# The four loads of a coming head pair, issued at four points of a recurrence period

## The chip, the cores and the metric

The kernel runs on one core of one Trainium2 chip. The metric is the device time of a launch in microseconds, from the core's own counters; smaller is better. Engines are named as in the profile: PE is TensorE, DVE is VectorE, ACT is ScalarE, POOL is GpSimd, SP is SyncE, whose queue issues nearly all DMAs here.

## The reference, cut to what matters

Two residual layers over x of 512 tokens by 1024 channels, float32. Layer 0 mixes by a convolution module and differential attention, layer 1 by a bidirectional RWKV-7 recurrence; each layer adds a cross attention into 256 memory tokens and a squared-ReLU MLP of 4096. The change lies in the recurrence of layer 1:

```python
def step(S, inp):
    r_t, w_t, k_t, v_t, a_t, b_t = inp
    sa = jnp.einsum('bhij,bhj->bhi', S, a_t)
    S = S * w_t[:, :, None, :] + sa[..., None] * b_t[:, :, None, :] + v_t[..., None] * k_t[:, :, None, :]
    return S, jnp.einsum('bhij,bhj->bhi', S, r_t)

y_f = wkv7_scan(r, decay[0], k_dir[0], v, -kk, kk * a_rate[0], reverse=False)
y_b = wkv7_scan(r, decay[1], k_dir[1], v, -kk, kk * a_rate[1], reverse=True)
```

There are 16 heads of 64 channels, and a forward and a backward scan.

## The kernel before

All other stages are dense products with weights streamed from HBM. The recurrence (`stage_wkv`) is done in chunks of 64 tokens, and for two heads at a time: a pair p (0 to 7) is 128 channels, one partition each. Before this stage r, the normalised k (called kk), k and v of all pairs have been written to HBM. `load_pair` (L1988 to L1991) brings the four 128x512 tiles of one pair into `pin[:, p % 2, a, :]`, with a = 0 for r, 1 for kk, 2 for k and 3 for v. Each tile is one DMA of 256 KB, and each raises the semaphore `s_pin[p % 2]` by 16. Two pairs have room at a time.

The work of a pair is spread over three periods. `SCAN_PERIOD` is a list of steps, each with a lag: in period t, the step "QB-1" is QB of pair t - 1 and "VT-0" is VT of pair t. `scan_order` (L2012) writes the list out, and every engine runs through the same order and does its own steps of it, in order. Steps in capitals are PE's. Steps in small letters that bear the name of a PE step take its result out of PSUM: ua, ub, vt on ACT, qb and bn on DVE. The steps that matter here, in PE's order within a period:

- UB-2, W-0, HK-2, GA-2, Z00-1, GB-2, HU-2, QB-1, Z01-1, X00-1, C1-2, X01-1, VT-0, TK-1, TB-1, Z11-1 and on. Z and X are the products of the blockwise inverse of pair t - 1, C1 to C6 the chunk chain of pair t - 2.
- VT (L2295 to L2302) centres and transposes v of pair t: eight matmuls with v of `pin` as weights. Ahead of it PE waits for the whole pair:

```python
elif kind == "VT":
    pe.wait_ge(s_half, 1)
    pe.wait_ge(s_pin[b], 64 * (p // 2 + 1))
```

- ua-2 and ub-2 (ACT, L2540) come at the beginning of the period. qb-1 (DVE, L2665) comes in the order right before VT-0.
- d0-0 and d2-0 (DVE, L2596 and L2630) read r and kk later in the period, d1 (L2619) reads k at the beginning of the next, bs (POOL, L2256) reads r and bn (DVE, L2646) reads v still later. d0, d1 and d2 wait for the same count of `s_pin` as VT.
- QB is `s_k_scores` in the rows, and its copy qb is the DVE instruction `s_k_scores<-ps,con` of L2665. VT is `ps<-s_centre,pair_in` of L2300.

SP's queue in period t (`scan_sp`), in order: at vt-0 it waits for vt, and for Y of pair t - 2, which PE ends with YS near the end of the period; then it issues four v_rows DMAs (L2209), four small lora loads (L1985), the store of y of pair t - 2 (L2221), and at bn-1 the store of the bonus of pair t - 1 (L2214) and the four loads of pair t + 1 (L1991). The tiles of pairs 0 and 1 are loaded ahead of the stage, all four together.

Of the kernel before, what the change touches and what calls it, by code (L numbers as in the profile page):

```python
# [30 lines left out]
C = D // P  # L31
# [74 lines left out]
class Kernel:  # L106
# [43 lines left out]
    def sb(self, name, shape, ctx=None, dt=F32):  # L150
        return (ctx or self.ctx).enter_context(self.nc.sbuf_tensor(name, shape, dt))
# [1456 lines left out]
def stage_rwkv_in(k):  # L1608
# [4 lines left out]
    with ExitStack() as cx:  # L1613
# [52 lines left out]
        def rin_sp(sp):  # L1666
            sp.dma_start(k.d_memt, k.memt[:, :, :]).then_inc(s_mtout, 16)
            k.load_weights(sp, sm + 4)
            sp.dma_start(k.d_h, h[:, :, :]).then_inc(s_hout, 16)
            k.load_weights(sp, at_end)  # L1670
            sp.wait_ge(s_hout, 16)
            sp.wait_ge(s_mtout, 16)

            sp.wait_ge(s_x, 48)
            sp.dma_start(k.mv_t[:, :, :], k.d_memt).then_inc(k.s_mv_in, 16)
            sp.dma_start(k.mv_w[:, :, :], k.i["xattn_w_kv"][1][:, 2 * D - SLOT:2 * D].rearrange("(k p) n -> p k n", p=P)) \
              .then_inc(k.s_mv_in, 16)
            for p in range(2):
                load_lora(k, sp, p)
            for c in range(8):  # L1680
                k.wait_freed(sp, num[("v", c)])
                sp.dma_start(k.d_v[:, c, :], sv[:, c % 2, :]).then_inc(s_vout[c % 2], 16)
                if c in (2, 5):
                    half = slice(4 * (c // 3), 4 * (c // 3) + 4)
                    sp.wait_ge(s_kk, half.stop)
                    sp.dma_start(k.d_kk[:, half, :], kk[:, half, :]).then_inc(s_kout, 16)
                elif c in (3, 4):

                    p = c - 3
                    k.wait_full(sp, num["k", 7])  # L1690
                    sp.wait_ge(s_kout, 16)
                    sp.wait_ge(s_out[p], 16 * 5)
                    sp.wait_ge(s_vout[p], 16)
                    load_pair(k, sp, p)
# [285 lines left out]
def load_lora(k, sp, p):  # L1980

    halves = (slice(0, CH), slice(CH, P))
    for a, src in enumerate((k.i["rwkv_w2"], k.i["rwkv_a2"])):
        for z in range(2):
            sp.dma_start(k.lora[halves[z], p % 2, a, :], src[0, z, :, p * P:(p + 1) * P]).then_inc(k.s_lora[p % 2], 16)  # L1985


def load_pair(k, sp, p):  # L1988

    for a, src in enumerate((k.d_r, k.d_kk, k.d_k, k.d_v)):  # L1990
        sp.dma_start(k.pin[:, p % 2, a, :], src[:, p, :]).then_inc(k.s_pin[p % 2], 16)  # L1991


# [63 lines left out]
def stage_wkv(k, proj):  # L2057
# [10 lines left out]
    with ExitStack() as cx:  # L2068
# [13 lines left out]
        ua = sb("a_rows_u", [P, NC, 2, 2, CH])  # L2082
# [67 lines left out]
        def full(eng, kind, p):  # L2150

            j = job[kind, p]
            eng.wait_ge(s_full[j % 2], j // 2 + 1)

        def taken(eng, kind, p):

            j = job[kind, p]
            eng.wait_ge(s_taken[j % 2], j // 2 + 1)

        def last_of(kinds, p):  # L2160
            return max(kinds, key=lambda n: job[n, p])
# [28 lines left out]
        def scan_sp(sp, gate):  # L2190
            for wait in k.scan_inputs:

                sp.wait_ge(*wait)
            for kind, p in order:
                if kind == "mv":
                    if p == 7:
                        sp.wait_ge(s_mvt, 2)
                        sp.dma_start(k.d_vv[1][:, :, 3 * SLOT:D], mvs).then_inc(s_mvo, 16)
                elif kind == last_of(("W", "A"), p) and p + 2 < C:
                    full(sp, kind, p)  # L2200
                    load_lora(k, sp, p + 2)
                elif kind == "vt":
                    taken(sp, "VT", p)
                    if p >= 2:
                        full(sp, "Y", p - 2)
                        sp.wait_ge(s_hf, p - 1)
                    for z in range(2):
                        for e in range(2):
                            sp.dma_start(vr[HP[z], p % 2, e::2].rearrange("p c h t -> p c (h t)"), vs[HP[e], :, :]) \  # L2209
                              .then_inc(s_vd, 16)  # L2210
                elif kind == "bn":
                    taken(sp, "BN", p)
                    if p < C - 1:
                        sp.dma_start(k.d_bon[:, p, :], bon[:, :]).then_inc(s_bo, 16)  # L2214
                    if p + 2 < C:
                        full(sp, "VT", p)
                        load_pair(k, sp, p + 2)
                elif kind == "ya":
                    if p < C - 1:
                        taken(sp, "Y", p)  # L2220
                        sp.dma_start(k.d_y[:, p, :], yb[:, p % 2, :]).then_inc(s_yo[p % 2], 16)  # L2221
                elif kind == "ly":
                    for b in range(2):
                        sp.wait_ge(s_yo[b], 32 if p == 0 else 64 - 16 * b)
                    gate.load_y(sp, p)
                elif kind == "lb":
                    taken(sp, last_of(("GA", "GB"), p + 6), p + 6)
                    sp.wait_ge(s_bo, 64 if p == 0 else 112)
                    gate.load_bonus(sp, p)
                elif kind == "lg":  # L2230
                    full(sp, "BN", 7)
                    gate.load_g2(sp)
                elif kind == "lw":
                    if p == 2:
                        taken(sp, last_of(("GA", "GB"), 7), 7)
                    elif p == 3:
                        gate.wait_g2(sp)
                    k.load_weights(sp, gate.first + p)
# [335 lines left out]
        def scan_dve(dve, gate):  # L2574
# [9 lines left out]
            for kind, p in order:  # L2584
# [122 lines left out]
                elif kind[0] == "c":  # L2707
# [5 lines left out]
                    else:  # L2713
# [4 lines left out]
                                      view(ends, 0, [[1, 2], [0, CH]]), ALU.mult).then_inc(s_sn, 1)  # L2718

    return Scan(proj, [x for x in order if x not in LEAD], scan_sp, scan_pe, scan_act, scan_dve, scan_pool, bon, lambda eng: taken(eng, "Y", C - 1),  # L2720
                lambda eng: taken(eng, "BN", C - 1), lambda eng: eng.wait_ge(s_y0, C))

# [246 lines left out]
```

## Time and profile before

| | |
|---|---|
| time, 3 runs | 1931.05 us median (1930.81 to 1932.45) |
| the profiled execution's own time | 1928.18 us |
| its span, first to last instruction | 1926.4 us |
| mean granted TensorE clock | 0.994 |
| PE busy | 1859.2 us (97%) |
| DVE busy | 1055.7 us (55%) |
| the stretch from 980 to 1380 us, with the recurrence | PE 384.8 of 400 us, DVE 309.2 us |

The span is one execution on the chip. A busy PE counts matmuls whose ends are modelled, so that it may hold short waits. "issue" as a releaser means that nothing in the profile explains the wait. DMA queue q1 holds all DMAs that SP issued, q8 and q14 the loads of instructions.

### The profile page before, as it was taken

How to read it: one execution, taken by the hardware profiler on the slowest of the kernel's cores; microseconds unless marked ns; L12 is line 12 of the kernel's file. 1: busy time of each engine (PE TensorE's matmuls, PEld its weight loads, DVE VectorE, ACT ScalarE, POOL GpSimd, SP SyncE). 2: the span in 40 equal slices, each digit the busy share in tenths (PEclk: the TensorE clock that was granted, in tenths of full speed). 3: DMA queues.
4: the chain of work that ended last, by engine and by line, in shares of the span. 5: the costliest groups of instructions: out<-in, count | busy, mean ns of one | idle time of the engine just before them, and what ended most of it. 6: DMA issues, size and time to landing. Idle time of an engine off the chain costs nothing.

```text
span 1926.4 us, 38666 instructions
## 1 busy us (share of the span) xinstructions
PE 1859.2 (97%) x17053; PEld 1529.8 (79%) x17053; DVE 1055.7 (55%) x1405; ACT 755.4 (39%) x1006; POOL 174.2 (9%) x136
## 2 busy tenths in 40 slices
PE   6999899999999999999999999999999999999997
PEld 4898558778888888775679898899787788888886
DVE  5897665444432443447648888787664344324422
ACT  4434674334421332323844343343643353213322
POOL 1000002000000000210003211111120010000000
PEclk9999999999999999999999999999999999999999
DMA  6227223112332232443441111112352132332221
GB/s 213 84 72 233 77 99 131 66 44 91 106 110 87 88 110 90 153 137 126 153 140 50 50 50 51 50 47 69 125 197 88 33 99 87 110 103 88 94 88 44
DMA packets 165503, 189.41 MB, mean 98 GB/s; under 512 B 11801, under 2 KB 152646, under 8 KB 163674
## 3 DMA queue, kind: packets, MB, share of 16 engines
q1 hardware_dynamic: 162016, 174.44, 28.2%
q0 software_dynamic: 3088, 12.45, 1.6%
q8 instruction: 135, 2.21, 0.5%
q14 instruction: 30, 0.25, 0.0%
q10 hardware_dynamic: 234, 0.06, 0.0%
HBM read 161.22 MB, written 21.51 MB: 95 GB/s over the span
## 4 chain that ended last, share of the span: by engine, by line
PE 48%; DVE 5%; issue 2%; ACT 2%; DMA 0%; ACTq 0%; DVEq 0%; SPq 0%
PE ps L357 10%; PE ps L359 10%; PE ps L358 10%; PE ps L2353 7%; PE ps L2319 2%; PE ps L2366 2%; PE ps L2307 1%; PE ps L1743 1%; PE ps L2330 1%; PE ps L1313 1%; PE ps L2412 1%; PE ps L2449 1%; PE ps L1294 1%; DVE s_inverse_t L2683 1%; PE ps L2286 1%
## 5 line engine op out<-in xcount | busy, mean ns | idle before, releaser
L344 DVE TENSOR_TENSOR weights_split<-w,weights_split 128x2048 fp32r<-128x2048 f32 x116 | 265.7, 2290 | 235.3 <-ACT weights_split L326 230.5
L326 ACT ACTIVATE weights_split<-w 128x2048 fp32r<-128x2048 f32 x118 | 225.5, 1911 | 288.7 <-PE ps L359 270.2
L357 PE MATMUL ps<-x_hn_hi,weights_split 128*128 128x512 f32 x640 | 252.7, 395 | 0.0
L359 PE MATMUL ps<-x_hn_hi,weights_split 128*128 128x512 f32 x640 | 249.2, 389 | 0.0
L358 PE MATMUL ps<-x_hn_lo,weights_split 128*128 128x512 f32 x640 | 249.0, 389 | 0.0
L357 PE MATMUL ps<-f_hidden_hi,weights_split 128*128 128x512 f32 x512 | 199.3, 389 | 0.0
L359 PE MATMUL ps<-f_hidden_hi,weights_split 128*128 128x512 f32 x512 | 199.2, 389 | 0.0
L358 PE MATMUL ps<-f_hidden_lo,weights_split 128*128 128x512 f32 x512 | 199.2, 389 | 0.0
L1563 DVE SCALAR_TENSOR_TENSOR f_relu<-ps,x_squares 128x512 f32<-128x512 f32 x64 | 44.1, 691 | 191.1 <-PE ps L359 172.5
L358 PEld LDWEIGHTS ps<-x_hn_lo,weights_split 128*128 128x128 f32 x640 | 120.2, 188 | 26.2 <-issue 1.4
L357 PEld LDWEIGHTS ps<-x_hn_hi,weights_split 128*128 128x128 f32 x640 | 120.2, 188 | 26.0 <-issue 1.4
L359 PEld LDWEIGHTS ps<-x_hn_hi,weights_split 128*128 128x128 f32 x640 | 120.1, 188 | 25.3
L462 POOL TENSOR_TENSOR x_squares<-x_squares 128x512 f32<-128x512 f32 x36 | 50.5, 1401 | 948.3 <-ACT x_squares L454 947.6
L1447 ACT ACTIVATE f_squared<-f_relu 128x512 f32<-128x512 f32 x64 | 40.4, 631 | 200.7 <-DVE f_relu L1563 200.7
L358 PEld LDWEIGHTS ps<-f_hidden_lo,weights_split 128*128 128x128 f32 x512 | 96.1, 188 | 20.1
L359 PEld LDWEIGHTS ps<-f_hidden_hi,weights_split 128*128 128x128 f32 x512 | 96.1, 188 | 19.9
L357 PEld LDWEIGHTS ps<-f_hidden_hi,weights_split 128*128 128x128 f32 x512 | 96.1, 188 | 19.7
L357 PE MATMUL ps<-x_src_hi,weights_split 128*128 128x512 f32 x256 | 103.9, 406 | 4.3 <-DVE weights_split L344 3.0
L359 PE MATMUL ps<-x_src_hi,weights_split 128*128 128x512 f32 x256 | 99.9, 390 | 0.0
L358 PE MATMUL ps<-x_src_lo,weights_split 128*128 128x512 f32 x256 | 99.7, 390 | 0.0
L357 PE MATMUL ps<-r_mix_hi,weights_split 128*128 128x512 f32 x192 | 79.2, 412 | 5.8 <-issue 3.3
L2265 POOL TENSOR_TENSOR s_levels<-s_b_scores_rows,con 128x1024 f32<-128x1024 f32 x24 | 56.4, 2362 | 277.5 <-DVE s_inverse L2678 170.0
(365 smaller groups left out, 3513.6 us busy)
## 6 DMA issues: line engine op xcount, KB each, us to landing
w<-in_ffn_w_up_dram SPq DMA_DIRECT2D x32, 1024.0 KB, 5.4
w<-in_ffn_w_down_dram SPq DMA_DIRECT2D x32, 1024.0 KB, 4.8
w<-in_xattn_w_kv_dram SPq DMA_DIRECT2D x15, 1024.0 KB, 5.5
w<-in_ab_w_in_dram SPq DMA_DIRECT2D x10, 1024.0 KB, 5.0
w<-in_xattn_w_q_dram SPq DMA_DIRECT2D x8, 1024.0 KB, 4.9
w<-in_xattn_w_o_dram SPq DMA_DIRECT2D x8, 1024.0 KB, 4.7
w<-in_ab_w_out_dram SPq DMA_DIRECT2D x4, 1024.0 KB, 5.3
w<-in_rwkv_w_r_dram SPq DMA_DIRECT2D x4, 1024.0 KB, 6.5
```

Source lines behind the costliest of these rows:

```text
L326: act.activation(hi, raw, ACT.Copy).then_inc(k.w_hi_ready, 1)
L344: eng.tensor_tensor(lo, raw, hi.bitcast(F32), ALU.subtract).then_inc(k.w_lo_ready, 1)
L357: pe.matmul(out, lhs[0], rhs[0], start=start, stop=False)
L358: pe.matmul(out, lhs[0], rhs[1], start=False, stop=False)
L359: return pe.matmul(out, lhs[1], rhs[0], start=False, stop=stop)
L462: pool.tensor_tensor(self.acc, former, self.sq[:, c % 2, :], ALU.add).then_inc(self.s_acc, 1)
L1447: act.activation(r2[:, n % 2, :], rl[:, n % 2, :], ACT.Square).then_inc(s_r2, 1)
L1563: dve.scalar_tensor_tensor(rl[:, n % 2, :], k.bank(up[half] + n), 0.0, rs, ALU.max, ALU.mult) \
L2265: pool.tensor_tensor(lm[:, l - 1], bb[:, p % 2, :, :, 0, :], over(k.mask(f"Z{l}"), NC, 2), ALU.mult) \
L2319: m = pe.matmul(bank(kind, p, h)[HP[z], i * P:(i + 1) * P], kb[r, u, c, z, :], ar[r, b, :, c, z, :], start=True, stop=True)
L2353: m = pe.matmul(k.ps[r, 6 + h, at(c)], lhs, rhs, start=True, stop=True)
L2366: m = pe.matmul(bank(kind, p, h)[r, i * P:(i + 1) * P], xt[r, h, c, :], ra[r, c, h, :, :].rearrange("p a t -> p (a t)"), start=True, stop= ...
```

## The change

`load_pair` takes a list of rows. At bn of pair p only v (row 3) of pair p + 2 is still loaded. kk (row 1) of pair p + 2 is issued when ACT has taken UA of pair p, r (row 0) when it has taken UB of pair p, and k (row 2) of pair p + 1 when DVE has taken QB of pair p. With the lags this means that v of pair t is issued at the end of period t - 1, and kk, r and k of pair t in period t, at ua-2, ub-2 and qb-1. The waits of the readers are not changed.

```diff
-def load_pair(k, sp, p):
-
-    for a, src in enumerate((k.d_r, k.d_kk, k.d_k, k.d_v)):
+def load_pair(k, sp, p, rows=range(4)):
+
+    for a in rows:
+        src = (k.d_r, k.d_kk, k.d_k, k.d_v)[a]
         sp.dma_start(k.pin[:, p % 2, a, :], src[:, p, :]).then_inc(k.s_pin[p % 2], 16)
@@ scan_sp
                     if p + 2 < C:
                         full(sp, "VT", p)
-                        load_pair(k, sp, p + 2)
+                        load_pair(k, sp, p + 2, [3])
+                elif kind in ("ua", "ub", "qb"):
+
+                    q = p + 1 if kind == "qb" else p + 2
+                    if 2 <= q < C:
+                        taken(sp, kind.upper(), p)
+                        load_pair(k, sp, q, [{"ua": 1, "ub": 0, "qb": 2}[kind]])
```

## Rows read from the trace of the kernel before

**Rows 1.** The page: engines busy over the whole span.
```profile
PE 1859.2 (97%) x17053; PEld 1529.8 (79%) x17053; DVE 1055.7 (55%) x1405; ACT 755.4 (39%) x1006; POOL 174.2 (9%) x136
```
**Rows 2.** Busy time by stretch, from one VT to the next: length, engines, PEclk, DMA share, GB/s.
```profile
1055.74:1102.83 47.09, 44.29 (x1295) 41.05 (x1292) 38.27 (x56) 17.72 (x23) 11.30 (x7) 1.00 0.19 51
1102.83:1147.62 44.79, 44.08 (x1295) 41.09 (x1293) 37.28 (x56) 17.61 (x23) 7.59 (x5) 1.00 0.20 53
1147.62:1193.82 46.20, 44.00 (x1295) 41.02 (x1293) 38.30 (x56) 17.73 (x23) 10.92 (x6) 1.00 0.18 52
1193.82:1242.36 48.54, 45.31 (x1296) 42.57 (x1293) 37.39 (x56) 17.61 (x23) 11.82 (x7) 0.96 0.19 50
1242.36:1287.71 45.35, 44.20 (x1295) 41.25 (x1292) 37.29 (x56) 17.61 (x23) 6.28 (x5) 1.00 0.18 50
```
**Rows 3.** The chain of waits from 1147 to 1194 us, its start: start, us, what.
```profile
1146.99 0.70 PE ps L2353 x23
1147.69 1.09 PE ps L2300 x8
1148.78 1.79 PE ps L2307 x16
```
**Rows 4.** SP's queue in order of time, end of one period.
```profile
1137.66 0.45 SPq L1991 DMA_DIRECT2D pair_in<-d_r  x1
1139.14 0.49 SPq L1991 DMA_DIRECT2D pair_in<-d_v  x1
```
**Rows 5.** DVE in order of time: qb ahead of the first and the last VT.
```profile
1054.22 1.22 DVE L2665 TENSOR_TENSOR s_k_scores<-ps,con 128x1024 f32<-128x1024 f32 x1
1285.50 1.22 DVE L2665 TENSOR_TENSOR s_k_scores<-ps,con 128x1024 f32<-128x1024 f32 x1
```
**Rows 6.** PE in order of time: VT of pairs 2 and 7, as far as each window went.
```profile
1055.74 0.71 PE L2300 MATMUL ps<-s_centre,pair_in 128*128 128x128 f32 x4
1287.71 0.71 PE L2300 MATMUL ps<-s_centre,pair_in 128*128 128x128 f32 x4
```
**Rows 7.** Landing of the first r (977.8 us, alone), then of the 32 lora loads.
```profile
DMA to landing us min/median/max: 2.7/2.7/2.7
...
DMA to landing us min/median/max: 2.0/2.7/7.3
```
**Rows 8.** Landing times of all four loads of one pair (issued 1091.6 to 1093.1).
```profile
DMA to landing us min/median/max: 3.5/4.0/6.3
```
**Rows 9.** ACT in order of time: ua and ub of one period.
```profile
1136.01 1.02 ACT L2540 ACTIVATE s_a_rows_u<-ps 128x1024 f32<-128x1024 f32 x1 [4.94 <-PE ps L2366]
1137.76 1.02 ACT L2540 ACTIVATE s_a_rows_u<-ps 128x1024 f32<-128x1024 f32 x1 [0.72 <-PE ps L2366]
```
**Rows 10.** PE in order of time: its long pauses between two VTs.
```profile
1097.83 0.64 PE L2398 MATMUL ps<-s_a_rows_u,s_b_scores_rows 64*64 64x64 f32 x29 [1.99 <-issue]
1190.52 0.32 PE L2319 MATMUL ps<-s_ar,s_kb 64*64 64x128 f32 x1 [1.33 <-issue]
1236.62 0.27 PE L2398 MATMUL ps<-s_a_rows_u,s_b_scores_rows 64*64 64x64 f32 x1 [2.65 <-issue]
```
**Rows 11.** DMA queues from 1102.83 to 1147.62 us: queue, packets, MB, share of 16 engines.
```profile
q1 hardware_dynamic: 2272, 2.23, 18.3%
q8 instruction: 10, 0.16, 1.5%
```
**Rows 12.** The same from 1227.5 to 1234.1 us (q8 had none).
```profile
DMA packets 889, 1.32 MB, mean 200 GB/s; under 512 B 115, under 2 KB 286, under 8 KB 889
...
q1 hardware_dynamic: 889, 1.32, 72.4%
```
**Rows 13.** Busy time by stretch: the burst; QB to VT at full clock, and after 2.65 us.
```profile
1094.00:1096.00 2.00, 1.85 (x78) 1.73 (x74) 1.97 (x4) 0.33 (x1) 0.45 (x1) 1.00 0.89 288
...
1143.30:1147.62 4.32, 4.31 (x136) 4.10 (x137) 3.76 (x6) 0.00 (x0) 4.24 (x4) 1.00 0.03 9
...
1236.74:1242.36 5.62, 5.62 (x138) 5.55 (x138) 2.11 (x3) 0.00 (x0) 5.54 (x4) 0.70 0.03 7
```
**Rows 14.** Waits of DVE from 1055.74 to 1335 us: for whom, us, times, longest.
```profile
DVE s_states L2716 <- PE ps L2412: 20.3, 12, 2.6
DVE s_b_scores_rows L2665 <- PE ps L2319: 12.4, 12, 1.9
```
**Rows 15.** PE in order of time: the wait for DVE that every period has.
```profile
1171.12 1.15 PE L2353 MATMUL ps<-s_inverse,s_b_scores_rows 64*64 64x64 f32 x32 [0.40 <-DVE s_inverse_t L2683]
```

## The prediction

> **What bounds the kernel now.** I read the page first: PE is busy 97% of the span and no other engine over 55% [rows 1], so what PE does not do while it could is lost. Then the stretches from one VT to the next: PE works 44.0 to 45.3 us of periods of 44.8 to 48.5 us [rows 2]. The recurrence is therefore bound by PE's own order; DVE, busy some 38 us, is the one that waits for PE [rows 2, 14]. In the chain of waits VT stands on the path with its neighbours touching it on both sides: nothing releases it but the matmul before [rows 3]. A delay put right ahead of VT falls on the path.
>
> **What the change does to VT.** VT waits for the full count of `s_pin`, that is for all four tiles, though it reads v alone. Before, the last of the four was issued at 1139.14 and VT began at 1147.62 [rows 2, 4]: 8.5 us for a load that lands in 3.5 to 6.3 us [rows 8]. The wait was never seen. After, k of the pair is issued only once qb is done, and qb comes in the order right before VT. So VT begins no sooner than the end of qb, plus the landing of one 256 KB load.
>
> The end of qb against the beginning of VT, for the six pairs that are loaded this way (2 to 7): for pair 2 qb ends at 1054.22 + 1.22 = 1055.44 and VT begins at 1055.74, 0.30 us later; for pair 7 it is 1285.50 + 1.22 = 1286.72 and 1287.71, 0.99 us [rows 5, 6]. The four between them have the same pattern, with 0.64, 0.16, 0.16 and 0.87 us. Together 3.1 us of slack. SP is idle at that point: its next wait, vt-0, comes after VT, so it issues the load at once.
>
> The landing: the trace has no 256 KB load issued into an idle queue in a period. The nearest is the first r before the stage, alone in the queue, 2.7 us; lora loads of 32 KB take from 2.0 us, the four loads in a burst have a median of 4.0 [rows 7, 8]. I take 2.7, as the load of k will stand alone too, with 2.0 and 4.0 as the ends. The stall is then 6 x 2.7 - 3.1 = **+13.1 us** (ends: 6 x 2.0 - 3.1 = +8.9 and 6 x 4.0 - 3.1 = +20.9).
>
> Is it given back later in the period? PE waits for DVE once in each period before the Z4 products, 0.40 us [rows 15] and 0.17 us right behind. But DVE gets there by way of the chain steps of L2716, for each of which it waits for PE [rows 14]; so DVE moves along with PE and I take nothing back. Everything behind VT in PE's queue (TK, TB, the Z and X products, the chain) moves by the whole stall, and ACT and DVE wait that much longer for it.
>
> **kk, r and v.** At bn SP still issues the bonus store and v. ua and ub end at 1137.03 and 1138.78, while the four loads went out from 1137.66 on, one each 0.5 us [rows 9, 4]. So kk follows v at once, and r after ub, at about 1138.8: at this place three of the four remain one burst, as late as before. They land by about 1143, 4 us ahead of VT: no cost. The three new waits of SP hold back nothing, for between ub and vt-0 its queue has no other step. d0, d1 and d2 come after VT, and see nothing new. Three SP waits and no added DMA: 0 us; without SP's idle time each would cost the 0.5 us of an issue.
>
> **What the shorter burst gives.** PE has three long pauses that no engine explains, 1.99, 1.33 and 2.65 us, all just before QB [rows 10]. In a quiet period the instruction queue q8 brings a packet each 4.5 us (10 in 44.79 us) [rows 11]; in the 6.6 us ahead of the longest pause it brought none, while q1 filled 72% of the 16 engines [rows 12]. I read these pauses as instruction loads that came late behind the burst of stores and loads. Without k the burst is 262 KB shorter, at 288 GB/s [rows 13] 0.9 us. Three pauses shorter by 0.9 give -2.7 us (ends: 0, if the burst is not their cause, and -6.0, if all go).
>
> **The clock.** After the 2.65 us pause the granted clock was 0.70 of full from QB to VT, that is partly at 1.2 instead of 2.4 GHz, and that piece took 5.62 us where it takes 4.32 us at full clock [rows 13]: 1.3 us. After the pause of 1.99 us the stretch kept 1.00 [rows 2, 10]. With the first pause at 1.75 us this 1.3 us goes (-1.3). But the stalls ahead of VT would be 2.40, 2.06, 2.54, 2.54, 1.83 and 1.71 us: three lie between the length that kept the clock and the one that lost it. I count half of them, 1.5 x 1.3 = +2.0 us (ends 0 and 6 x 1.3 = 7.8).
>
> **Sum:** +13.1 - 2.7 - 1.3 + 2.0 = **+11.1 us**. From the profiled execution's 1928.18 (span 1926.4 and 1.8 around it) this gives 1939.3; the median of the runs stands 2.9 higher, at 1931.05, so that the forecast is **1942.2 us**.
>
> **A rule of the skill on the pauses.** The Trainium skill, "DMA: Bandwidth & Descriptors", section "Queues, rings and completion order", says that each DMA engine serves the queues that have work in turn, a packet at a time. By this rule an instruction packet would not wait for the burst to drain, the shorter burst would give nothing, and the sum would be rival 3's. The rows speak against it (no q8 packet in the whole burst), though they don't show when the packet was asked for.
>
> **Rivals.**
> 1. *Not slower: the stall eats PE's idle time.* If PE's pauses and waits are not rigid but time in which it waits for DVE or for its instructions, a stall at VT lets these catch up. In the five periods PE is idle 2.80, 0.71, 2.20, 3.23 and 1.15 us, 2.0 a period [rows 2], 12.1 us for six. If all of it goes, 13.1 - 12.1 = +1.0, so 1932 us, no measurable difference. It decides when the time from VT to the next VT is set by something that does not pass through VT. For: the idle time is there. Against: DVE waits for PE at the chain steps, and the pauses lie 40 us behind VT. Chance 0.10.
> 2. *The landing is long.* A 16 KB instruction load or the restart of the DMA engines beside it makes k land in 4.0 us, and the pauses, now 3.0 to 3.8 us, cost the clock each time: +20.9 - 4.0 + 7.8 = +24.7, 1955.8 us. For: loads in bursts take that long. Against: nothing else is in the queue then (share 0.03 before VT, rows 13). Chance 0.13.
> 3. *The pauses before QB stay.* They come from when the instructions are asked for, not from the burst: +13.1 + 2.0 = +15.1, 1946.2 us. For: the quiet second period has the same burst and no pause [rows 2]. Chance 0.18.
> 4. *The pauses go whole.* 13.1 - 6.0 - 1.3 + 2.0 = +7.8, 1938.9 us. For: the pauses come only in some periods, so a little may decide. Against: three of four loads and both stores still form the burst. Chance 0.13.
>
> That the loads are not spread as the words of the change say is part of the forecast: only k leaves the burst.
>
> **How the numbers follow.** The forecast has 0.46. The differences that a measurement of this kernel can tell start at 0.2%, 3.9 us: the forecast and rivals 2, 3 and 4 lie above it, rival 1 within. With the lower ends (landing 2.0, pauses gone) 8.9 - 7.3 = +1.6 would be within too, and a little of rival 1 beyond: faster 0.03, same 0.09, slower 0.88. The range runs from 1935 (between rivals 1 and 4) to 1953 (short of rival 2): it leaves out most of these two, some 2 in 10.
>
> **What would show it.** After the change: a wait of PE ahead of L2300 for the DMA of `pair_in`, six times, 1.7 to 2.6 us each, with the k load issued right after the DVE row of `s_k_scores`, and landing in 2.7 us; kk and r issued within 2 us of v; periods of 47 to 49 us; the pauses before L2319 shorter than 2 us; a granted clock under 1.00 in one or two of the periods. Wrong if PE has no wait before L2300, if DVE and not PE is found waiting less in each period, or if the pauses before QB are gone and PE's idle time in a period is no larger than before.

## The result, and the profile after

The changed kernel takes 1951.2 us in the median of 4 runs (1947.95 to 1954.49), against 1931.75 us of the kernel before: ratio 1.0096, with an interval of 1.0077 to 1.0116. That is 19.5 us slower; 11.1 had been forecast, in a range whose upper end (1953) lies 1.8 us above the measured time. In a later comparison (a_after_again, below) it was 1.0099 (1.0085 to 1.0113), 1952.5 against 1932.95 us.

The profiled execution is the slowest of the four: 1954.49 us, span 1952.7 us, mean clock 0.988. VT of pair 0, ahead of anything that was changed, starts at 1003.8 in it and started at 1000.5 before. So 3.3 of the 26.3 us between the two spans lie ahead of the change. The profile of before, on the other hand, is of an execution 2.9 us under its median: what the two profiles differ by is more than the kernels do.

PE by page, to compare with [rows 1]:
```profile
PE 1868.4 (96%) x17053; PEld 1538.4 (79%) x17053; DVE 1055.2 (54%) x1405; ACT 755.4 (39%) x1006; POOL 173.7 (9%) x136
```
The same instructions, and 9.2 us more of busy time at a mean granted clock of 0.988 for 0.994. Whom PE waited for, from 1050 to 1350 us (us, times, longest), before, then after:
```profile
PE ps L2398 <- issue: 4.6, 2, 2.7
PE ps L2353 <- DVE s_inverse_t L2683: 3.4, 12, 0.4
PE ps L2319 <- issue: 1.3, 1, 1.3
...
PE ps L2353 <- issue: 0.6, 2, 0.5
```
```profile
PE ps L2307 <- DMA pair_in<-d_k: 14.2, 6, 2.6
PE ps L2405 <- issue: 5.3, 3, 2.4
PE ps L2360 <- DVE s_inverse_t L2690: 3.5, 12, 0.4
PE ps L2360 <- issue: 1.7, 4, 0.7
PE ps L2326 <- issue: 1.3, 1, 1.3
```
The changed kernel's lines are numbered 7 higher here: L2307 is VT, L2405 and L2326 are L2398 and L2319 of before. The wait for the load of k is new: six times, 14.2 us. The twelve waits for DVE ahead of the Z and X products are what they were (3.4 us, then 3.5); waits without a releaser at those products rose from 0.6 to 1.7 us. How one of the six comes about, DVE, SP and PE in order of time in the period of pair 4:
```profile
1156.08 1.22 DVE L2672 TENSOR_TENSOR s_k_scores<-ps,con 128x1024 f32<-128x1024 f32 x1
```
```profile
1146.61 0.45 SPq L1992 DMA_DIRECT2D pair_in<-d_v  x1
1147.10 0.45 SPq L1992 DMA_DIRECT2D pair_in<-d_kk  x1
1148.38 0.32 SPq L1992 DMA_DIRECT2D pair_in<-d_r  x1
1157.32 0.32 SPq L1992 DMA_DIRECT2D pair_in<-d_k  x1
```
```profile
1156.39 1.15 PE L2360 MATMUL ps<-s_product,s_inverse_t 64*64 64x64 f32 x32
1160.15 1.13 PE L2307 MATMUL ps<-s_centre,pair_in 128*128 128x128 f32 x8 [2.62 <-DMA pair_in<-d_k]
```
qb ends at 1157.30, SP issues k at 1157.32, the load lands 2.7 us later, and VT starts at 1160.15, though v has been there for long. The other three loads still go out within 1.8 us of each other. Landing of the six k loads: 2.6, 2.8, 2.7, 2.6, 3.1 and 3.6 us.

The stretches from one VT to the next, which answer to [rows 2] (length, then PE, PEld, DVE, ACT, POOL busy, granted clock, DMA share, GB/s):
```profile
1061.42:1112.43 51.01, 45.51 (x1293) 42.54 (x1293) 38.60 (x57) 17.61 (x23) 11.13 (x6) 0.97 0.18 47
1112.43:1160.15 47.72, 44.11 (x1292) 41.09 (x1293) 37.50 (x57) 17.61 (x23) 8.26 (x5) 1.00 0.19 50
1160.15:1209.28 49.13, 44.18 (x1293) 41.20 (x1293) 38.09 (x57) 17.61 (x23) 10.70 (x6) 1.00 0.19 49
1209.28:1261.25 51.97, 46.94 (x1293) 44.03 (x1293) 37.05 (x56) 17.72 (x23) 9.46 (x5) 0.93 0.18 47
1261.25:1311.30 50.05, 45.67 (x1293) 42.83 (x1293) 37.74 (x57) 17.72 (x23) 8.98 (x5) 0.97 0.17 45
```
The five have grown from 231.97 to 249.88 us, by 3.92, 2.93, 2.93, 3.43 and 4.70. The two with 2.93 kept the full clock: the stalls in them, 2.62 and 2.51 us, are nearly all of their growth. In the other three the clock is 0.93 to 0.97, once 0.96 before, and PE's busy time in all five is 4.5 us longer. The pauses before QB, which answer to [rows 10]:
```profile
1103.73 0.64 PE L2405 MATMUL ps<-s_a_rows_u,s_b_scores_rows 64*64 64x64 f32 x29 [2.26 <-issue]
1203.39 0.32 PE L2326 MATMUL ps<-s_ar,s_kb 64*64 64x128 f32 x1 [1.31 <-issue]
1253.36 0.27 PE L2405 MATMUL ps<-s_a_rows_u,s_b_scores_rows 64*64 64x64 f32 x1 [2.38 <-issue]
```
5.95 us in sum, 5.97 before: the forecast had 2.7 us less. (The lists above have 5.9 us at these two lines before and 6.6 after, where a short pause of 0.65 us has come ahead of pair 7.) The 4 us after each stall at VT, and after the first and last of these pauses, show where the clock went (it is the first number after POOL's):
```profile
1061.42:1065.42 4.00, 4.00 (x62) 3.78 (x64) 3.88 (x4) 2.54 (x3) 1.65 (x1) 1.00 0.01 4
1112.43:1116.43 4.00, 4.00 (x63) 3.78 (x65) 2.75 (x4) 2.54 (x3) 0.00 (x0) 1.00 0.00 0
1160.15:1164.15 4.00, 4.00 (x62) 3.78 (x64) 3.45 (x4) 2.54 (x3) 1.22 (x1) 1.00 0.00 0
1209.28:1213.28 4.00, 4.00 (x23) 4.00 (x24) 2.73 (x4) 1.62 (x2) 0.00 (x0) 0.63 0.02 4
1261.25:1265.25 4.00, 4.00 (x21) 4.00 (x22) 3.16 (x4) 1.06 (x2) 0.00 (x0) 0.57 0.00 0
1311.30:1315.30 4.00, 4.00 (x24) 3.73 (x24) 2.80 (x4) 1.62 (x2) 0.50 (x1) 0.68 0.00 0
1103.73:1107.73 4.00, 4.00 (x103) 3.99 (x104) 0.57 (x3) 0.00 (x0) 3.92 (x3) 0.60 0.01 4
1253.36:1257.36 4.00, 4.00 (x94) 4.00 (x96) 1.50 (x3) 0.00 (x0) 3.92 (x3) 0.67 0.02 4
```
Five losses of clock in the recurrence, where the profile of before has one. The number changes from one execution to the next: the profile of a_after_again, the same kernel, has four. At VT the stalls of 2.09, 2.50 and 2.62 us kept it and those of 2.51, 2.08 and 2.44 us lost it: in this range the length of the stall does not decide.

### The profile page after: what moved, and what is told of

The parts are those of the page before. It is cut to its first block, busy times and chain, and to the rows that moved or that the text cites. A ratio compares the mean times of both kernels' runs of the same rounds, so it can differ in the third digit from the quotient of the medians.

```text
span 1952.7 us, 38666 instructions
## 1 busy us (share of the span) xinstructions
PE 1868.4 (96%) x17053; PEld 1538.4 (79%) x17053; DVE 1055.2 (54%) x1405; ACT 755.4 (39%) x1006; POOL 173.7 (9%) x136
## 4 chain that ended last, share of the span: by engine, by line
PE 47%; DVE 5%; issue 2%; ACT 2%; DMA 2%; SPq 0%; ACTq 0%; DVEq 0%
PE ps L357 10%; PE ps L359 9%; PE ps L358 9%; PE ps L2360 6%; PE ps L2326 2%; PE ps L2314 1%; PE ps L2373 1%; PE ps L1743 1%; DMA pair_in<-d_k 1%; PE ps L2337 1%; PE ps L1313 1%; PE ps L2293 1%; PE ps L2419 1%; PE ps L1294 1%; DVE s_inverse_t L2690 1%
```

## The experiments

Each was run against the kernel before on the same chip. Its ratio is that of the runs, with a 95% interval. The experiments come from three such comparisons, with a median of the kernel before of 1933.1 us (b_own_v to f_at_QB), 1932.0 (g_at_x01, i_filler, h_own_quiet, j_stores_quiet) and 1932.95 us (a_after_again, k_filler_half, l_two_in_burst).

### Is it VT's wait for k?

**b_own_v**: v of pairs 2 to 7 counts on a semaphore that has done its work by then (`s_kout`, at 32), and VT waits for that.
```diff
-        sp.dma_start(k.pin[:, p % 2, a, :], src[:, p, :]).then_inc(k.s_pin[p % 2], 16)
+        sem = k.scan_inputs[4][0] if a == 3 and p >= 2 else k.s_pin[p % 2]
+        sp.dma_start(k.pin[:, p % 2, a, :], src[:, p, :]).then_inc(sem, 16)
@@ VT
-                    pe.wait_ge(s_pin[b], 64 * (p // 2 + 1))
+                    if p < 2:
+                        pe.wait_ge(s_pin[b], 64)
+                    else:
+                        pe.wait_ge(k.scan_inputs[4][0], 32 + 16 * (p - 1))
@@ d0, d1, d2
-                    dve.wait_ge(s_pin[b], 64 * (p // 2 + 1))
+                    dve.wait_ge(s_pin[b], 64 + 48 * (p // 2))
```
Expected: 

> The changed kernel, but the loads of v count on a semaphore of their own, and VT waits for v alone; all four loads stay at their new places, and d0, d1 and d2 still wait for r, kk and k. Theory 1 (the cost is VT's wait for the landing of k, 14.2 us, and the clock that its pauses cost): the wait of PE ahead of VT is gone, the granted clock has one dip in the recurrence at most, and the time is that of the kernel before, 1931 +- 2 us, ratio 0.999 to 1.001. Theory 2 (the spread loads themselves cost, by the three waits of SP, or by loads beside the work of the engines): the time stays at 1945 to 1951 us. Theory 3 (the three pauses before QB come from the burst): they are 0.5 to 1 us shorter each and the time is 1927 to 1929 us.

Measured: 1932.1 us, ratio 0.9998 (0.9987 to 1.0010). Its waits of PE, 1050 to 1350 us:
```profile
PE ps L2409 <- issue: 4.5, 3, 2.0
PE ps L2364 <- DVE s_inverse_t L2694: 3.4, 12, 0.4
PE ps L2330 <- issue: 2.2, 1, 2.2
```
No row of VT (L2311) is left, and the whole 19.5 us are gone with all four loads at their new places. The wait is the cause; the places alone cost nothing. The pauses before QB did not shrink (third theory, not with three loads in the burst). One expectation failed: the profiled execution, the slowest of twelve (1935.96 us), lost the clock three times and not once at most, after the pauses of 1.99, 2.23 and 1.83 us.

**c_k_back**: k is loaded at bn again, kk and r stay at ua and ub.
```diff
-                        load_pair(k, sp, p + 2, [3])
+                        load_pair(k, sp, p + 2, [2, 3])
-                elif kind in ("ua", "ub", "qb"):
+                elif kind in ("ua", "ub"):
```
Expected: 

> The changed kernel with k loaded at bn again, beside v; kk and r stay at ua and ub. Theory 1 (only k's place costs): 1931 +- 2 us, ratio 0.999 to 1.001, no wait of PE ahead of VT. Theory 2 (each of the loads that was moved costs something): 1935 to 1945 us.

Measured: 1929.7 us, ratio 0.9986 (0.9975 to 0.9998). Theory 1: kk and r cost nothing where they are, and perhaps give a little. All four loads still leave together at the end of the period here, and the longest pause before QB is
```profile
1238.21 0.27 PE L2405 MATMUL ps<-s_a_rows_u,s_b_scores_rows 64*64 64x64 f32 x1 [2.87 <-issue]
```
The granted clock was 1.00 over the 4 us after it, and the profile shows no loss of clock in the recurrence.

**d_k_alone**: the reverse, only k is moved.
```diff
-                        load_pair(k, sp, p + 2, [3])
+                        load_pair(k, sp, p + 2, [0, 1, 3])
-                elif kind in ("ua", "ub", "qb"):
+                elif kind == "qb":
```
Expected: 

> The kernel before with k alone moved to qb; kk and r are loaded at bn with v. Theory 1: the whole cost of the change, ratio 1.008 to 1.012, with six waits of PE ahead of VT of 2.1 to 2.6 us each. Theory 2 (the places of kk and r carry part of it): ratio under 1.006.

Measured: 1952.6 us, ratio 1.0101 (1.0081 to 1.0121), with this wait (1050 to 1380 us):
```profile
PE ps L2307 <- DMA pair_in<-d_k: 14.8, 6, 2.8
```
k's place is the whole cost. The longest of the six waits, 2.8 us, is a little over what was expected.

### Does the cost follow from when k is issued?

**f_at_QB**: SP waits for the end of QB on PE, 3 us earlier, for k alone.
```diff
-                        taken(sp, kind.upper(), p)
+                        (full if kind == "qb" else taken)(sp, kind.upper(), p)
```
Expected: 

> The changed kernel, but k is issued when PE has ended QB, and not when DVE has taken it, some 3 us earlier (QB ends at 1144.4 and qb at 1147.5 in the period of pair 4 of the kernel before). Theory 1 (the stall is the end of the wait plus one landing of 2.7 us, less the slack): the six waits ahead of VT fall from 2.4 us to under 0.3 us each, no clock is lost to them, and the time is 1931 to 1933 us. Theory 2 (a third wait of SP and a single load in mid-period cost whatever their place is): still over 1940 us.

Measured: 1931.7 us, ratio 0.9999 (0.9988 to 1.0010), and one wait is left of six:
```profile
PE ps L2307 <- DMA pair_in<-d_k: 0.8, 1, 0.8
```
It is the wait ahead of VT of pair 5, where a pause of PE of 1.33 us in the middle of QB lets QB end late. The rest of the theory holds.

**g_at_x01**: k is issued when DVE has ended the step after qb.
```diff
-                        taken(sp, kind.upper(), p)
+                        if kind == "x01":
+                            sp.wait_ge(s_it[1], 10 * p + 2)
+                        else:
+                            taken(sp, kind.upper(), p)
```
Expected: 

> The changed kernel, but k is issued when DVE has ended x01, the next step after qb, 1.7 us later (1149.16 against 1147.46 in the period of pair 4 of the kernel before, less in periods with more slack). Theory 1 (each microsecond of the issue of k stands ahead of VT six times, and the longer pauses cost the clock in each period): the waits ahead of VT sum to 22 to 25 us and the time is 1960 to 1966 us, 10 to 14 us over the changed kernel. Theory 2 (something else in the period takes up a part of the stall): under 1956 us.

Measured: 1965.4 us, ratio 1.0177 (1.0155 to 1.0198), and:
```profile
PE ps L2310 <- DMA pair_in<-d_k: 25.5, 6, 4.3
```
From 14.2 to 25.5 us of wait, the time rose from 1951.2 to 1965.4 us: 14.2 us for 11.3, so all of the wait and some clock (mean granted clock of the runs 0.985, for 0.990). Nothing in the period takes up a part of it. The size is rough, as each wait is read from the slowest execution of its kernel. The wait was a little over what was expected (22 to 25).

### What are the 5 us over the wait?

**i_filler** and **k_filler_half**: products of the identity with itself ahead of PE's wait at VT, so that PE works while it would stand still. They write where VT writes afterwards.
```diff
+                    s = bank(kind, p, 0)
+                    if p >= 2:
+                        for i in range(16):
+                            pe.matmul(s[:, (i % 4) * P:(i % 4 + 1) * P], k.ident, k.ident, start=True, stop=True)
                     pe.wait_ge(s_pin[b], 64 * (p // 2 + 1))
```
Expected of i_filler: 

> The changed kernel with 16 products of the identity with itself, 128x128 each, ahead of PE's wait at VT for pairs 2 to 7, written where VT writes afterwards. They take 1.9 us of the stall of 2.4 (VT's own eight take 1.0 to 1.2) and leave the result alone. Theory 1 (of the 19.5 us, 14.2 are the wait and 5 the clock that the six pauses cost): no dip of the granted clock at a VT, the waits left ahead of VT sum to 2 to 4 us, and the time is 1946 to 1948 us, 3 to 5 us under the changed kernel. Theory 2 (the part over 14.2 us is not the clock): the time stays at 1951 us.

Measured: 1951.3 us, ratio 1.0097 (1.0078 to 1.0115). The row of PE in one period:
```profile
1106.46 3.84 PE L2308 MATMUL ps<-con 128*128 128x128 f32 x32
```
Sixteen products are 32 records and 3.8 us, longer than the stall. The wait for k is gone from the list, and so is the clock's loss (1.00 over the 4 us from each of the six VTs on, and no loss in the recurrence), but the filler cost as much. As a test of the clock it was undecided, so it was made again with half.

**k_filler_half**, `range(8)` for `range(16)`, beside **a_after_again**, the changed kernel as it is.

Expected of k_filler_half: 

> i_filler with 8 products of the identity for 16. In i_filler each product was two matmul records of 0.115 us, and the 16 took 3.7 us, more than the stall; 8 take 1.85 us and leave 0.3 to 0.7 us of it. Theory 1 (14.2 us are the wait and some 5 the clock): waits left ahead of VT 1.5 to 4 us in sum, no dip of the granted clock at a VT, and a time 3 to 5 us under the changed kernel run beside it. Theory 2 (the clock is not what the rest is): the same time as the changed kernel within 1.5 us.

Expected of a_after_again: 

> The changed kernel once more, beside the two below: ratio 1.008 to 1.012, 1950 to 1953 us, waits of PE ahead of VT that sum to 14 to 15 us.

Measured: 1948.6 us, ratio 1.0078 (1.0065 to 1.0092), against 1952.5 and 1.0099 (1.0085 to 1.0113) of the changed kernel. Each filler took 2.05 us. Waits of PE for k, 1050 to 1350 us, in a_after_again, then in k_filler_half:
```profile
PE ps L2307 <- DMA pair_in<-d_k: 15.4, 6, 2.8
```
```profile
PE ps L2311 <- DMA pair_in<-d_k: 3.5, 3, 1.7
```
The 15.4 us are a little over the 14 to 15 expected. The fillers do no work that the result needs, and k is still issued after qb; yet the kernel is 3.9 us faster. The granted clock is 1.00 over the 4 us after each VT, where the changed kernel lost it after two of six here; one loss is left in the recurrence, after a pause before QB. The busy time and granted clock (column before the last two) from 1050 to 1320 us, of a_after_again and of k_filler_half:
```profile
1050.00:1320.00 270.00, 241.31 (x6905) 225.57 (x6897) 201.75 (x303) 93.86 (x122) 56.80 (x30) 0.97 0.17 45
```
```profile
1050.00:1320.00 270.00, 254.71 (x7173) 237.84 (x7166) 207.83 (x312) 98.57 (x129) 56.88 (x30) 0.99 0.17 45
```
That is the part of the cost that is clock. (The busy times do not compare: the two windows hold different amounts of work, and one the fillers.) The intervals of the two ratios overlap a little (1.0085 against 1.0092), but all five runs with fillers (up to 1949.3 us) are faster than all four without (from 1950.7). The size, 3.9 us, is rough. An estimate from all runs of this comparison agrees: the mean granted clock was 0.99250 before, 0.99075 after the change and 0.99340 with the fillers, and the differences, 0.00175 and 0.00265 of some 1950 us, are 3.4 and 5.2 us.

The fillers show one thing more. They lengthen PE's stream of instructions and leave the burst as it is, and the pauses moved. Ahead of VT of pair 4, where before has none, after has 0.29 us and no other run more than 1.14, k_filler_half has one of 2.23 us and i_filler this:
```profile
1152.88 1.10 PE L2330 MATMUL ps<-s_ar,s_kb 64*64 64x128 f32 x32 [2.67 <-issue]
```
So which period has a pause depends on where PE is in its instructions, and not on the DMAs alone.

### Do the pauses before QB come from the burst?

**h_own_quiet**: b_own_v, and kk, r and k are all issued at qb. v alone stays in the burst.
```diff
-                elif kind in ("ua", "ub", "qb"):
+                elif kind == "qb":
 
-                    q = p + 1 if kind == "qb" else p + 2
+                    q = p + 1
...
-                        load_pair(k, sp, q, [{"ua": 1, "ub": 0, "qb": 2}[kind]])
+                        load_pair(k, sp, q, [1, 0, 2])
```
Expected: 

> VT waits for v alone, on a count of its own; kk, r and k all are issued at qb, where the queue is empty, so that the burst at the end of the period holds the two stores and v alone (786 KB for 1573 KB). Theory A (the pauses before QB, 6 us in three periods of the kernel before, are instruction loads behind the burst): they are gone or under 0.7 us each, no dip of the clock, ratio 0.995 to 0.997. Theory B (they come from when the instructions are asked for, whatever the other DMAs do): pauses of 1.3 to 2.7 us in three periods as before, ratio 0.999 to 1.001.

Measured: 1924.6 us, ratio 0.9959 (0.9944 to 0.9975): faster than both kernels. From one VT to the next:
```profile
1056.09:1102.01 45.92, 44.46 (x1296) 41.28 (x1293) 37.99 (x56) 17.73 (x23) 9.65 (x6) 1.00 0.19 53
1102.01:1146.84 44.83, 43.95 (x1296) 41.04 (x1293) 37.83 (x56) 17.73 (x23) 9.01 (x6) 1.00 0.20 53
1146.84:1191.67 44.83, 43.97 (x1296) 41.01 (x1293) 38.23 (x56) 17.72 (x23) 9.51 (x6) 1.00 0.20 54
1191.67:1236.94 45.27, 43.97 (x1295) 41.09 (x1292) 38.23 (x56) 17.72 (x23) 9.94 (x6) 1.00 0.20 53
1236.94:1282.31 45.37, 44.21 (x1295) 41.32 (x1292) 37.88 (x56) 17.72 (x23) 9.57 (x6) 1.00 0.18 50
```
Set beside [rows 2], the same work and the same DMAs take 226.22 us for 231.97, all at full clock; the undisturbed 44.8 us of one period before is now nearly the rule. The longest pause of [rows 10], 2.65 us, has become this:
```profile
1232.27 0.27 PE L2409 MATMUL ps<-s_a_rows_u,s_b_scores_rows 64*64 64x64 f32 x1 [0.46 <-issue]
```

**j_stores_quiet**: h_own_quiet, and the stores of the bonus (pairs 0 to 5) and of y (0 to 4) are issued at qb too.
```diff
-                    if p < C - 1:
+                    if p == C - 2:
                         sp.dma_start(k.d_bon[:, p, :], bon[:, :]).then_inc(s_bo, 16)
...
                         load_pair(k, sp, q, [1, 0, 2])
+                        sp.dma_start(k.d_bon[:, p - 1, :], bon[:, :]).then_inc(s_bo, 16)
+                        if p >= 2:
+                            taken(sp, "Y", p - 2)
+                            sp.dma_start(k.d_y[:, p - 2, :], yb[:, p % 2, :]).then_inc(s_yo[p % 2], 16)
                 elif kind == "ya":
-                    if p < C - 1:
+                    if C - 4 < p < C - 1:
```
Expected: 

> As h_own_quiet, and the stores of the bonus and of y are issued at qb too, behind the loads, for all but the last pairs, so that near QB only v, the v_rows and the lora loads move. Theory A: no pause over 0.5 us before QB in the periods of pairs 3 to 7, ratio 0.994 to 0.996. Theory B: the pauses as before, ratio 0.999 to 1.001.

Measured: 1925.0 us, ratio 0.9965 (0.9952 to 0.9979), the same as h_own_quiet and just outside what was expected. The pauses before QB are no more than 0.66 us (0.5 expected), but one of 1.96 us has come after it:
```profile
1242.97 1.55 PE L2368 MATMUL ps<-s_product,s_inverse_t 64*64 64x64 f32 x46 [1.96 <-issue]
```
That fits a burst that now goes out at qb; it was not followed further.

**l_two_in_burst**: h_own_quiet with kk back at bn.
```diff
-                        load_pair(k, sp, p + 2, [3])
+                        load_pair(k, sp, p + 2, [3, 1])
-                        load_pair(k, sp, q, [1, 0, 2])
+                        load_pair(k, sp, q, [0, 2])
```
Expected: 

> As h_own_quiet, but kk is loaded at bn with v: the burst holds two loads and two stores. h_own_quiet with one load gave 0.996, b_own_v with three 1.000. Theory A (the pauses before QB are an instruction load that comes late by what the burst holds): between them, ratio 0.996 to 0.999, pauses of 0.5 to 1.5 us. Theory B (what helped h_own_quiet was something else, such as the waits of SP at ua and ub that it does not have): 0.996, as with one load.

Measured: 1929.1 us, ratio 0.9978 (0.9967 to 0.9989). The pause by that same instruction, in l_two_in_burst and in b_own_v:
```profile
1234.22 0.27 PE L2409 MATMUL ps<-s_a_rows_u,s_b_scores_rows 64*64 64x64 f32 x1 [0.95 <-issue]
```
```profile
1241.88 0.27 PE L2409 MATMUL ps<-s_a_rows_u,s_b_scores_rows 64*64 64x64 f32 x1 [1.83 <-issue]
```
With one, two and three loads in the burst the pause is 0.46, 0.95 and 1.83 us, and the kernels, all without a wait at VT, stand at 0.9959, 0.9978 and 0.9998. The intervals of neighbours overlap, those of one and three loads do not. The 1.83 us are the lowest of what three loads gave: the same pause was 2.38 us after the change, 2.58 in a_after_again, 3.13 in d_k_alone and 3.43 in f_at_QB. With four it was 2.65 before and 2.87 in c_k_back. All pauses of this kind from 1050 to 1350 us, in l_two_in_burst, then in h_own_quiet:
```profile
PE ps L2409 <- issue: 1.9, 3, 1.0
...
PE ps L2330 <- issue: 0.8, 1, 0.8
```
```profile
PE ps L2409 <- issue: 1.1, 2, 0.6
```
1.1, 2.7 and, in b_own_v, 6.7 us; with four loads 5.9 before and 5.5 in c_k_back. So the pauses are short with one or two loads, and between three and four there is no difference to see: that the burst has a part in them is shown, that they grow with its size beyond that is not. All waits of PE without a releaser in this stretch, wherever they stand, are 3.1 us with one load, 6.6 with two and 9.7 in b_own_v, but 6.5 before. That what is late behind the burst is PE's instructions is likely and not shown. Ahead of the three pauses of before, of 1.99, 1.33 and 2.65 us, the instruction queue q8 brought no packet for 6.9, 6.1 and 7.2 us, and the fillers moved the pauses; but h_own_quiet has such a gap too, of 6.0 us, with a pause of 0.62 behind it, and in the changed kernel gaps of 8.1 to 10.1 us stand around four of the six stalls at VT, with no more than one 256 KB load running, so that a gap can also follow from a stop of PE.

## Why the prediction was right, and where it was not

- **VT waits for k, though it reads v**: right. Six waits, SP issuing within 0.03 us of the end of qb; b_own_v and d_k_alone settle it from both sides.
- **Landing 2.7 us, slack 3.1, sum +13.1**: 14.2 us measured (15.4 and 14.8 in two more profiles), so 1.1 us too low. Four of the six loads landed in 2.6 to 2.8 us, two in 3.1 and 3.6: 17.4 in sum for 16.2.
- **Nothing is given back in the period**: right. The waits for DVE ahead of the Z and X products stayed, the two periods at full clock grew by 2.93 us each for stalls of 2.62 and 2.51, and g_at_x01 paid for its extra wait in full. Rival 1 falls.
- **kk, r and SP's waits at 0 us**: right (b_own_v 0.9998, c_k_back 0.9986).
- **The shorter burst, -2.7 us**: this step failed. It took the pause to shrink by k's share of the bytes, and the pauses kept their 5.95 us. The result was rival 3's, but not all of its reason, that the burst has no part in them: two loads fewer took over half of the pauses away, and h_own_quiet most of the rest. The other half of that reason, that they hang on when PE asks for its instructions, fits the pauses that moved with the fillers.
- **The rule on queues in the Trainium skill**, "DMA: Bandwidth & Descriptors", section "Queues, rings and completion order", has each DMA engine serve its queues in turn, a packet at a time. The prediction took from it that a shorter burst gives nothing. For the change itself that gave the better figure (+15.1), but for bursts as a whole that conclusion does not hold: in h_own_quiet and l_two_in_burst, with fewer loads in the other queue, the pause by the same instruction fell to 0.46 and 0.95 us, from 1.83 or more with three. Whether the queues are served in turn no run here shows: nobody saw when an instruction packet was asked for.
- **The clock, +0.7 us net (-1.3 for a pause that would shorten, +2.0 for half of three stalls at risk)**: mis-sized. Three of six stalls lost the clock, and two of the pauses before QB for one before: four losses more than before, 5.2 us at the 1.3 us apiece of [rows 13]; in a_after_again it is two stalls and two pauses, three losses more and 3.9 us. PE's busy time rose 4.5 us in the five periods, and k_filler_half, with PE kept at work, gave 3.9 us back. The term also has a slip of counting: of its own six stalls four, 2.40, 2.06, 2.54 and 2.54 us, lie between 1.99 and 2.65 us, not three, and half of four would be +2.6, the sum +11.7. The reading by length itself was wrong too: a pause of 1.83 us lost the clock (b_own_v), and one of 2.87 kept it (c_k_back). And the pause of 1.99 us, which it counted as safe, came back as 2.26 and lost it.
- **Sum**: 14.2 + 3.4 to 5.2 of clock + 0 of the pauses is near the measured 19.5; forecast 13.1 + 0.7 - 2.7 = 11.1. All three misses have one sign. Two thirds of the cost were foreseen by the right mechanism; that the rest still falls inside the range, 1.8 us under its end, is partly luck.

## What to carry to other kernels

When loads that share a semaphore count are issued at different points, every reader waits for the last of them: place the loads and split the count together, or the first reader pays a whole landing (2.6 to 3.6 us here) each time. Six stalls of 2 to 3 us on a PE that is otherwise full cost about a third more than their length (19.5 us for 14.2), as the clock falls after some of them. And a burst of loads is not free on an engine that never waits for them: with the count split and three of four loads moved to a quiet point, the idea of this change gives -0.4% (0.9944 to 0.9975).

## What the runs showed of the hardware

PE stood still for 1.3 to 2.7 us, with no releaser in the profile, when a burst of four 256 KB loads and two stores went out; ahead of these three pauses the queue of instruction loads brought no packet for 6.1 to 7.2 us, where 4.5 us are usual. One load fewer left the pauses as they were (6.7 us in sum in b_own_v, 5.9 before), two fewer made them 2.7 and three fewer 1.1 us. More PE instructions in each period, with the burst unchanged, moved a pause of 2.2 to 2.7 us into a period that had none. And PE's stalls of 2.1 to 2.6 us at one and the same place left the granted clock at full three times, and took it to 0.57 to 0.68 of full over the next 4 us three times, with no order by their length. In other profiles a pause of 1.83 us lost it (0.61) and one of 2.87 us kept it (1.00).
